# Router logits by token rows, LayerNorm affine steps moved into the second expert item, and the first expert started by halves

## The reference

```python
x = layer_norm(ALPHA * x + g_m * y, ln_w[layer, 0], ln_b[layer, 0])   # after the mixer
h = x * (1.0 + sc_f) + sh_f
y = moe_swiglu(h, w_router, b_router, w_up, w_down)
x = layer_norm(ALPHA * x + g_f * y, ln_w[layer, 1], ln_b[layer, 1])

logits = t @ w_router + b_router          # t: 256 x 1024, w_router: 1024 x 8
top_vals, top_idx = lax.top_k(logits, 2)
weights = jax.nn.softmax(top_vals, axis=-1)
out = out + combine[:, e:e + 1] * swiglu(t, w_up[e], w_down[e])       # for each expert e
```

## Time and profile before

| | |
|---|---|
| median of 3 runs | 1717.54 us (1715.79 to 1718.16) |
| profiled execution, own time | 1712.77 us |
| its span in the trace | 1710.9 us |
| TensorE busy | 1612.3 us |
| VectorE busy | 1285.5 us |
| ScalarE busy | 1008.8 us |
| POOL busy | 136.7 us |
| mean granted TensorE clock | 0.979 |

### The profile page before, as it was taken

How to read it: one execution, slowest core, us unless ns; L and a number is a source line. 1 busy time by engine, 2 the same in 40 slices (tenths; PEclk the granted TensorE clock), 3 DMA queues, 4 the chain that set the end, 5 groups by cost and what they waited for, 6 DMA issues and landing times.

```text
span 1710.9 us, 20084 instructions
## 1 busy us (share of the span) xinstructions
PE 1612.3 (94%) x7810; PEld 1291.3 (75%) x7810; DVE 1285.5 (75%) x1162; ACT 1008.8 (59%) x867; POOL 136.7 (8%) x92
## 2 busy tenths in 40 slices
PE   4987999999999999789999999999999999999996
PEld 1863766788867777578888888888888888888875
DVE  1383738655467665789898898898898888998987
ACT  1442225444344445357777777777777777777775
POOL 0420402020001001110000000000000000000004
PEclk9898999999999999889999999999999999999998
DMA  9459785965454444479999999999999999999994
GB/s 328 139 178 376 259 295 197 316 206 191 172 172 158 155 159 161 156 266 389 387 387 386 369 386 385 373 390 370 384 390 370 385 387 371 386 384 364 390 376 156
DMA packets 234370, 515.33 MB, mean 301 GB/s; under 512 B 8936, under 2 KB 40960, under 8 KB 234176
## 3 DMA queue, kind: packets, MB, share of 16 engines
q1 hardware_dynamic: 228272, 491.99, 78.6%
q0 software_dynamic: 3008, 10.20, 2.0%
q10 hardware_dynamic: 2992, 11.79, 1.9%
HBM read 507.15 MB, written 13.11 MB: 304 GB/s over the span
## 4 chain that ended last, share of the span: by engine, by line
PE 86%; DVE 7%; DMA 3%; issue 2%; ACT 2%; POOL 1%; POOLq 0%; SPq 0%; DVEq 0%
PE bank L759 25%; PE bank L761 25%; PE bank L760 25%; DMA ring<-in_cond_w 3%; PE bank L738 2%; PE bank L926 2%; PE bank L1190 1%; PE bank L754 1%; DVE arena L1793 1%; ACT w_part L1317 0%; DVE w_part L1652 0%; PE bank L1172 0%; DVE w_lo L1663 0%; PE bank L1181 0%; PE bank L771 0%
## 5 line engine op out<-in xcount | busy, mean ns | idle before, releaser
L1663 DVE TENSOR_TENSOR w_lo<-ring,w_hi 128x2048 fp32r<-128x2048 f32 x336 | 764.9, 2290 | 104.0 <-ACT w_hi L1546 102.4
L1546 ACT ACTIVATE w_hi<-ring 128x2048 fp32r<-128x2048 f32 x334 | 640.5, 1918 | 194.8 <-PE bank L761 190.4
L759 PE MATMUL bank<-w_lo,heT_hi 128*128 128x512 f32 x896 | 353.7, 395 | 3.8 <-DVE w_lo L1663 2.3
L761 PE MATMUL bank<-w_hi,heT_hi 128*128 128x512 f32 x896 | 349.7, 390 | 0.0
L760 PE MATMUL bank<-w_hi,heT_lo 128*128 128x512 f32 x896 | 348.9, 389 | 0.0
L1652 DVE TENSOR_TENSOR w_part<-ring,w_part 128x1024 fp32r<-128x1024 f32 x148 | 184.5, 1255 | 181.2 <-ACT w_part L1317 174.3
L1317 ACT ACTIVATE w_part<-ring 128x1024 fp32r<-128x1024 f32 (+1 forms) x162 | 168.9, 1049 | 233.5 <-PE bank L761 227.6
L759 PEld LDWEIGHTS bank<-w_lo,heT_hi 128*128 128x128 f32 x896 | 168.3, 188 | 39.0 <-issue 5.9
L761 PEld LDWEIGHTS bank<-w_hi,heT_hi 128*128 128x128 f32 x896 | 168.2, 188 | 35.9
L759 PE MATMUL bank<-w_part,hT_hi 128*128 128x512 f32 (+1 forms) x448 | 178.1, 398 | 17.8 <-DVE w_part L1652 12.3
L760 PEld LDWEIGHTS bank<-w_hi,heT_lo 128*128 128x128 f32 x896 | 168.4, 188 | 33.6
(11 more groups left out here) (342 smaller groups left out, 1586.3 us busy)
## 6 DMA issues: line engine op xcount, KB each, us to landing
ring<-in_moe_w_up SPq DMA_DIRECT2D x224, 1024.0 KB, 8.7
ring<-in_moe_w_down SPq DMA_DIRECT2D x112, 1024.0 KB, 7.8
ring<-in_cond_w SPq DMA_DIRECT2D x24, 2048.0 KB, 10.6
ring<-in_ffn_w_up SPq DMA_DIRECT2D x22, 1024.0 KB, 8.4
ring<-in_od_w_in SPq DMA_DIRECT2D x8, 2048.0 KB, 8.0
ring<-in_ev_w_in SPq DMA_DIRECT2D x5, 2048.0 KB, 12.5
ring<-in_ffn_w_down SPq DMA_DIRECT2D x5, 2048.0 KB, 7.6
ring<-in_od_w_in SPq DMA_DIRECT2D x8, 1024.0 KB, 7.9
```

Source lines behind the costliest of these rows:

```text
L759: mm(bank, lhs[0], rhs[1], start=start, stop=False)
L761: return mm(bank, lhs[0], rhs[0], start=False, stop=stop)
L1546: f(w_hi[:, n % 3], half_landed(act, it, u, half), ACT.Copy) \
L1663: tt(w_lo[:, buf], at, w_hi[:, buf].bitcast(F32), ALU.subtract).then_inc(S["w_lo"], 1)
```

## The change

Five edits.

1. The router's logits are made with the tokens held (128 x 128 blocks of `hT`) and the router weights streamed (8 columns): for each tile of tokens, eight blocks of three products. The logits come out as 128 tokens x 8, so `routerT`, its copy and the transposes go, and a tile's products wait only for that tile's blocks.
2. In `stage_end`, where no part is left over (stage 2, and any other without `part_left`), tile 1's scale is made ahead of tile 0's modulation, and the affine steps are no longer made there.
3. The affine steps of stage 2 are made in item 1, on VectorE, at units 3 and 5 (one tile each), behind the low parts of the next unit. POOL's load of the last LayerNorm's weights, which waits for them, comes behind the scatter of the rows; ScalarE waits for them ahead of its scaling of `xs` in the last item.
4. TensorE waits for the item's rows by halves, at its first unit, instead of for both at the end of the item before.
5. ScalarE rounds piece 2 of the first expert behind the exponential, and VectorE makes its low part behind that of piece 1; both are left out of the item.

On TensorE, before: the last transposes are those of `hs`, and the router begins with one wait on all four banks of `hT`.

```diff
--- before.py
+++ after.py
@@ -200,7 +200,7 @@
     o += [("od_out", t, i) for t in range(NT) for i in range(2)]
     o += [("ret_y", RH - 1, t) for t in range(NT)] + [("ret_yT", RH - 1, t) for t in range(NT)]
     o += [("cond", *key) for key in END_COND[2]] + [("hT", 4, i) for i in BY_TILE]
-    o += [("routerT",), ("router",), ("rank",)]
+    o += [("router",), ("rank",)]
     o += [("rows_T", 0), ("rows_T", 1)]
     return o
 
@@ -446,7 +446,6 @@
         code, cnt, over, rank_o, moved = mt(NE), mt(NE), mt(NE), mt(NE), mt(NE)
         slot_f, slot_c = mt(2, NT), mt(2, NT, NE)
         over_hot, over_id = mt(3, NE), mt(3)
-        logit_rows = mt(SEQ)[0:NE]
         first_hot = mt(NT, P)
 
         TWO_PARTS = ("ffn_up", "od_qk")
@@ -806,7 +805,7 @@
             def narrow(key, rows):
 
                 for i in range(4):
-                    taken(pe, "hT", {"ab": 0, "router": 4}[key], i)
+                    taken(pe, "hT", 0, i)
                 bank, full = to_fill(pe, key + "T")
                 for k in range(KC):
                     last = three(bank[0:NE, 0:SEQ], (nw_hi[:, k], nw_lo[:, k]), (hT_hi[:, k], hT_lo[:, k]),
@@ -1151,7 +1150,14 @@
             turn(4, h_ready(3), BY_TILE)
 
             pe.wait_ge(S["nw_lo"], 2)
-            narrow("router", logit_rows)
+            bank, full = to_fill(pe, "router")
+            for t in range(NT):
+                for k in range(KC):
+                    if k % 4 == 0:
+                        taken(pe, "hT", 4, k // 4 * 2 + t)
+                    last = three(bank[:, t * NE:(t + 1) * NE], [a[:, k, t * P:(t + 1) * P] for a in (hT_hi, hT_lo)],
+                                 (nw_hi[:, k], nw_lo[:, k]), k == 0, k == KC - 1)
+            last.then_inc(full, 1)
 
             pe.wait_ge(S["late_in"], 16)
             pe.wait_ge(S["rank_in"], 1)
@@ -1182,7 +1188,7 @@
                                   start=(t == 0), stop=(t == NT - 1))
                 last.then_inc(full, 1)
 
-            def item(it, last_one=False):
+            def item(it, last_one=False, first=False):
                 def act_turn(pair):
                     item_taken(pe, it, "up", 2 * pair + 1)
                     bank, full = item_to_fill(pe, it, "act_T", pair)
@@ -1199,6 +1205,8 @@
                 for u in range(N_UP):
                     bank, full = item_to_fill(pe, it, "up", u)
                     for half in range(2):
+                        if u == 0:
+                            taken(pe, "rows_T", half) if first else item_taken(pe, it, "rows_T", half, ago=1)
                         w = piece(u, half, lambda a: a.rearrange("p (k n) -> p k n", k=KC // 2))
                         for k in range(KC // 2):
                             kk = KC // 2 * half + k
@@ -1238,11 +1246,6 @@
                         elif i < N_DOWN - 1:
                             last.then_inc(S["down_units"], 1)
 
-                for half in range(2):
-                    item_taken(pe, it, "rows_T", half)
-
-            for half in range(2):
-                taken(pe, "rows_T", half)
             def finish(it):
 
                 finishing(pe, "hot_taken", it, 1, 1)
@@ -1258,7 +1261,7 @@
                 finish(it)
 
             for it in range(LAST_ITEM):
-                item(it)
+                item(it, first=(it == 0))
             count = over_count(pe)
             item(LAST_ITEM, True)
             finish(LAST_ITEM)
@@ -1508,11 +1511,10 @@
             turned(4, BY_TILE)
 
             for half in range(2):
-                if half:
-                    copy(("routerT",), logit_rows, lambda b: b[0:NE, 0:SEQ])
                 f(w_hi[:, half], half_landed(act, 0, 0, half), ACT.Copy).then_inc(S["w_hi"], 1)
             act.wait_ge(S["route_in"], 1)
             f(e12, e12, ACT.Exp).then_inc(S["route_exp"], 1)
+            f(w_hi[:, 2], half_landed(act, 0, 1, 0), ACT.Copy).then_inc(S["w_hi"], 1)
             for half in range(2):
                 bank, _ = filled(act, "rows_T", half)
                 f(heT_hi[:, 4 * half:4 * half + 4], heads(bank), ACT.Copy).then_inc(S["tok_hi"], 1)
@@ -1541,6 +1543,8 @@
 
                     for half in range(2):
                         n = 2 * u + half
+                        if n == 2 and not first and it == 0:
+                            continue
 
                         piece_read(act, it, n - 3)
                         f(w_hi[:, n % 3], half_landed(act, it, u, half), ACT.Copy) \
@@ -1554,6 +1558,7 @@
                         result(earlier)
                     if u in (RESULT_UNIT + 2, RESULT_UNIT + 4) and not first and it == LAST_ITEM:
                         t = (u - RESULT_UNIT - 2) // 2
+                        act.wait_ge(S["ln_done"], 3 * NT)
                         f(xs[:, t], xs[:, t], ACT.Copy, scale=ALPHA).then_inc(S["scaled"], 1)
                     if u < N_UP and u % 2 == 1:
 
@@ -1745,12 +1750,10 @@
                     turned(stage + 2, BY_TILE[2:], 2)
                 else:
                     moments(1)
+                    to_normalise(stage, 1)
                     modulated(0)
-                    to_normalise(stage, 1)
                     modulated(1)
                     turned(stage + 2, BY_TILE)
-                if not part_left:
-                    affines(stage)
 
             def affines(stage, tiles=range(NT)):
 
@@ -2111,6 +2114,7 @@
                     V.do(last)
             last.then_inc(S["hot_ready"], 1)
             rest(0, 1, 0, 1)
+            rest(0, 2, 1, 2)
             for half in range(2):
                 tokens_lo(half, filled(dve, "rows_T", half), 1 + half)
             dve.wait_ge(S["hot_ready"], 1)
@@ -2154,7 +2158,8 @@
             def item(it, first=False, earlier=None):
                 def split_unit(u):
                     for n in (2 * u, 2 * u + 1):
-                        rest(it, n, n // 2 % RING, n % 3)
+                        if n != 2 or first or it > 0:
+                            rest(it, n, n // 2 % RING, n % 3)
 
                 last = first or it == LAST_ITEM
                 if first:
@@ -2170,6 +2175,8 @@
                         tt(e_a, e_s, bank[:], ALU.mult).then_inc(free, 1)
                     if u < N_UNITS - last:
                         split_unit(u + 1)
+                    if not first and it == 1 and u in (3, 5):
+                        affines(2, ((u - 3) // 2,))
                     if 2 <= u <= N_UP and u % 2 == 0:
                         dve.wait_ge(S["act_hi"], it * N_PAIRS + u // 2)
                         bank, free = item_filled(dve, it, "act_T", u // 2 - 1)
@@ -2354,8 +2361,6 @@
             split_to("od_out", 2)
             fold(2, 1, 3)
             split_to("od_out", 3)
-            pool.wait_ge(S["ln_done"], 3 * NT)
-            load_ln(3)
 
             pool.wait_ge(S["slots_out"], 16 * FILLS)
             pool.wait_ge(S["picks_ready"], 1)
@@ -2365,6 +2370,8 @@
                     pool.indirect_dma_start(slots, pick(i, t), hs[:, t], None, bounds_check=N_BLOCKS * P - 1) \
                         .then_inc(S["slots_in"], 16)
 
+            pool.wait_ge(S["ln_done"], 3 * NT)
+            load_ln(3)
             pool.wait_ge(S["slots_in"], 16 * 2 * NT)
             pool.wait_ge(S["slots_out"], 16 * (FILLS + LAST_ITEM))
             split(pool, "w_lo", LAST_ITEM, 2 * (N_UNITS - 1 - RING) + 2)
```

## The result

Eight runs of the changed kernel have a median of 1721.63 us (1717.6 to 1723.13), eight of the kernel before on the same chip 1715.87 (1715.35 to 1718.16): the ratio of the two over these runs is 1.0022 (95% interval 1.0013 to 1.0031), 3.8 us slower, while the two medians by themselves lie 5.8 us apart. The forecast was +4.1 us, 1721.6 for the median. The changed kernel's profiled execution took 1720.55 us with a span of 1718.6 at a mean clock of 0.975; that of before 1712.77, 1710.9 and 0.979.

The account below looks back on a forecast made before the run. TensorE, 86% of the chain, was taken as the bound, except between the layer's last output product and the first expert. Router +2.1, first expert -2.4, affine steps +4.4 gave +4.1 us: median 1721.6, range for all 1716.2 to 1725.0.

Parts of the forecast that it names:

- Affine steps in the second item, +4.4: Item 1, units 3 and 5: VectorE makes gated rows late, stalling TensorE 2.1 and 2.3 us; bounds 0 and 4.9.
- the clock falls in a stall: Rival, item 1: low clock behind one or both stalls, 1.7 us each, sum +5.8 to +7.5; chance 0.18.
- First expert, -2.4: First expert's start: rows by halves and third piece ahead remove two TensorE waits, 2.4 us won; bounds 1.5 and 3.2.
- the first half alone: First expert: lower bound of the gain, 1.5 us, from waiting for the rows by halves only.
- Router and scale, +2.1: Layer's end to router's add: 48 products at 0.213 us bring the add 2.1 us later, 0.99 won included.
- the new ones run at the low clock too: Router on TensorE: all 48 new products run at clock 0.50, 0.213 us each, 10.24 us together.
- the edit of the scale, costed at 0.99: Layer's end on VectorE: tile 1's scale first starts tile 1's modulation at 712.67 instead of 713.66, 0.99 us won.
- The products wake the clock: Rival, router: after 16 products at 0.213, 32 at 0.107; add 1.3 us earlier, sum +0.7; chance 0.13.
- the row of 136.02: Evidence for the router's low clock: 32 products, 128x128 held, one column streamed, 4.10 us; the clock fell at 139.2.
- One pass of 0.107: Rival, router: a load takes 0.107 us at the low clock; add at 721.8, sum -1.0; chance 0.09.
- The affine steps hidden: Rival, item 1: VectorE's 0.85 us idle per unit absorbs the steps, stalls near nothing, sum -0.3; chance 0.08.
- The load in item 1 at nothing: Item 1: the last LayerNorm's 1 MB load, worth 2.7 us of transfer, was taken to cost nothing behind the stalls.

Follow-up runs that it names:

- e2: The changed kernel with the old router products (24, weights held, copy and two transposes): 1719.12 us, ratio 1.0008 to before.
- e1: The changed kernel with the affine steps back in the layer's end, the load still behind the scatter: 1718.26 us, ratio 1.0003 to before.
- e5: As e1, but with the last LayerNorm's weights loaded ahead of the scatter again: 1714.03 us, ratio 0.9981 to before.
- e6: The kernel before with only the affine steps, and the load that waits for them, moved into item 1: 1724.26 us, ratio 1.0041.
- e11: The changed kernel with the four affine operations one at a time at units 15 to 18 (down weights) of item 1: 1713.17 us, ratio 0.9979 to before.
- e10: As e5 without the third piece made ahead, rows still waited for by halves: 1718.78 us, ratio 1.0005 to before.
- e9: The kernel before with only tile 1's scale made ahead of tile 0's modulation: 1716.84 us, ratio 0.9990.
- e7: As e5 with 32 router products for 48, high tokens held once and both weight parts streamed: 1714.74 us, ratio 0.9986 to before.
- e8: As e5 with the old router products: 1714.80 us, ratio 0.9982 to before.
- e12: As e5 with the 48 router products made twice, the second set into columns nothing reads: 1723.91 us, ratio 1.0042 to before.
- e4: The kernel before with the first expert's part alone (halves, third piece ahead) and the load behind the scatter: 1718.96 us, ratio 1.0014.
- e3: The kernel before with tile 1's scale first, the first expert's part and the load behind the scatter: 1715.99 us, ratio 0.9989.

## Why the prediction held, step by step

**Affine steps in the second item, +4.4: right.** Place, mechanism and size were as forecast. e2 shows 2.19 + 2.34 = 4.5 us at full clock; e1 and e5 bring the steps home and the stalls are gone; e6 makes them alone. e11 shows that VectorE's work in the item is not the cause: the same four operations cost 0.7 us one at a time between down pieces, where no gated rows are due. It changed the place and the grouping together, and no run parts the two; that VectorE's lead over TensorE decides fits both and is not shown by itself. The rival "the clock falls in a stall" came true for the first of the two stalls in the changed kernel and in e6, and added its 1.7 us; in e2 it did not.

**First expert, -2.4: right, and only as a pair.** The gap between the picked rows and the first product (38.23 - 30.16 - 6.55 = 1.52 us before) is gone: 34.28 - 29.08 - 5.45 = -0.25, so 1.77 won. From the first product to the first turn it is 14.76 instead of 15.63, 0.87 won. Together 2.6. But the bound of 1.5 for "the first half alone" was wrong: e10 shows that alone it is worth nothing (its third piece starts 0.5 us later than that of e9, which has both waits). And 0.7 us goes back in item 0: the turns of pairs 2 and 3 stand 12.05 us apart instead of 11.37 (775.94 to 787.99), and ScalarE waits 8.1 us for weights instead of 4.4. The other kernels with the third piece made ahead and the load out of the way lose much the same (item 0 takes 119.2 to 119.4 in e5, e7, e8, e11 and e12, 118.9 in e2), those without it 0.3 at most (118.6 to 118.8 in before, e6, e9 and e10). An early start is not what counts, as e12 starts 10 us later than e5 and loses the same. The forecast had not asked what paces the weights. The net of this edit is -1.9.

**Router and scale, +2.1: the step that failed.** Measured -1.07. The step was "the new ones run at the low clock too: it is 0.50 until about 722.9 now". The price at the low clock was right, 0.213, and e12 measures it again over 48 products. But the edit of the scale, costed at 0.99 of VectorE's time, also closed the wait between the two turns, and that was enough for the clock to rise before the router's products (e9: 1.93 at the add for this edit alone, 2.70 on TensorE). In all eleven kernels with the scale ahead the clock is 1.00 again 15.4 to 15.9 us behind the layer's end; in the three without it (before, e4, e6) only at 22.2 to 22.6. Of the 48, 29 then took 0.111 us, and 19 the full 0.213. What would have been seen by asking: an edit that moves 16 transposes together changes what TensorE did ahead of the router, and the prediction carried the clock of before over unchanged. Against the old products, with the scale ahead and no affine steps before the add in both, the new ones cost 1.84 more at the add and 1.1 at the first expert product (e2), where 3.1 were expected by the forecast. Where the affine steps stand before the add they cover half of it: 0.86 at the add and 0.2 to 0.3 at the first expert product (e5 to e8).

**The rivals on the router.** "The products wake the clock" is not it, though its 1.3 us earlier at the add are near the 1.07 measured. The clock was at 1.00 already when they began and fell at 722.96 in an unbroken stream of them, as in the row of 136.02, and in e12 it stayed at 0.50 for 13 us of it. "One pass of 0.107" fails too: 0.111 is the price at clock 1.00 and 0.213 at 0.50, side by side in one stream. The Trainium skill ("TensorE: Matmul & The Clock Gate", LDWEIGHTS) gives a load its columns divided by 1.2 GHz and makes no difference by the clock, 107 ns for 128 columns. The trace agrees at 1.00, where a product with its load took 0.111 us, and not at 0.50.

**The affine steps hidden, and the load.** That rival is out: VectorE's 0.85 us of idle time lies ahead of the low parts after the change as well, and the turns waited. The load in item 1 at nothing was right: it was issued at 900.77, and the next pair lost 0.06 us. What nobody asked was what it costs elsewhere: behind the scatter in item 0 it costs 2.3 and 2.6 us in e3 and e4 and, with a fall of the clock, 3.5 in e1 (their item 0 against that of e5).

**The sum.** By marks, up to pair 3 of item 1: -1.07 at the add, -1.10 as the picked rows' products took 5.45 us instead of 6.55 (the clock rose at 32.5 from the layer's end, in before at 35.9), -2.64 for the first expert, +0.72 in item 0, +6.06 in item 1 (4.4 of stalls, 1.7 of clock). That is +1.97, and 208.50 - 206.54 = +1.96 was measured. Behind it come 0.6 in item 4 and the 1.6 of the last item: +4.2, which with the 3.5 ahead of the change makes the 7.7 us between the spans. The ratio says +3.8. So in this execution the sum of +4.1 was met by errors against each other, which is luck: up to the end of the picked rows the prediction was 4.3 us too dear and for the first expert 0.2, and it left out 4.6 us behind them (0.7 of weights, 1.7 of clock in item 1, priced as a rival, 0.6 and 1.6). The last two are not the change's: the fall at the last item stands in nine of the 14 executions, of kernels with and without each edit, and a loss like the 0.6 in one item stands in e8 (0.5 in item 3) and e11 (0.7 in item 2) as well. Without them the marks give +2.0; what makes it 3.8 over eight runs stays open.

Two slips of the prediction change nothing: three quarters of the forecast and the first rival are 0.57 and not 0.59, and +5.8 on 1717.54 is 1723.3 and not 1723.4.

## What to carry to other kernels

On an engine that is fully booked, ask of each place how far ahead of its reader it works: the same 4.9 us of VectorE's time cost 4.5 to 6 us in front of the gated rows, 0.7 among the down pieces, and ahead of the router's add nothing or 2.7, as the router was slow or fast. When an experiment comes out level, look which engine set the time, as in e7: what was made faster may stand behind something else. Two waits in a row are one: taking away the first (halves) only lengthens the second (third piece) until both are gone. And when an edit draws TensorE's work together or apart, the clock behind it has to be worked out anew; a clock read off the old trace belongs to the old gaps.

## What the runs showed of the hardware

- In all six kernels with 48 products of 128x128 held and 8 columns streamed the clock fell in the unbroken stream of them, 18.8 to 19.4 us behind the layer's end, and in e7 at the last of its 32, at 19.2; in the four with the old products and the scale ahead it was at 1.00 until 22.6 to 25.8. In e12 it stayed at 0.50 from 725 to 738 among such products. One costs 0.111 us at 1.00 and 0.213 at 0.50.
- Two lots of eight transposes with 0.56 us between them were followed by a rise of the clock, in eleven executions of eleven; with 2.30 us between them the clock was still 0.50 at 722 in before, and in e4 and e6 as far behind their layer's ends.
- After a wait of 2.0 to 2.3 us in a dense stream at 1.00 the clock fell in some executions and not in others: at the first stall of item 1 in two of three, at the second in none of three, at the wait of 2.32 us in the last item in nine of 14. Such a fall cost 1.6 to 1.7 us.
- A load of 1 MB on POOL's queue right behind the scatter made item 0 longer by 2.3 and 2.6 us (e3, e4) and by 3.5 with a fall of the clock (e1), all against e5, where it is ahead of the scatter; in item 1 it cost 0.06. Why was not settled: the sum of ScalarE's waits for weights does not tell them apart (7.0 to 11.1 us with it, 7.9 in e5), only a longer single wait does (2.3 to 3.1 against 2.1), and no run parts the load from the rows' own transfer.
- The same stretch of program ended between 700.7 and 707.3 us in the profiled executions, and the clock of its first 100 us, 0.88 to 0.95, explains only part of it: e7 ended it at 704.8 with 0.95, before at 700.7 with the same.
